# Joins kept clear of GpSimd, two norms in column halves, an earlier copy and count, a store in three parts

## The reference

```python
# layer 0
h = deltanet_mixer(x, ...)   # x @ w_in, conv of 4 taps, silu, a and b gates, chunked gated delta rule
x = layer_norm(ALPHA * x + h, g, b)                  # norm 0
h = (silu(x @ w_gate) * (x @ w_up)) @ w_down         # dense mixer, width 2816
x = layer_norm(ALPHA * x + h, g, b)                  # norm 1
# layer 1
k, v = x @ w_kv;  h = sliding_window_attention(x @ w_q, k, v) @ w_o
x = layer_norm(ALPHA * x + h, g, b)                  # norm 2
h = sum over the top 2 of 8 experts: gate * (silu(x @ w_g[e]) * (x @ w_u[e])) @ w_d[e]
x = layer_norm(ALPHA * x + h, g, b)                  # norm 3, the output

# in the delta rule: (I + L)^-1 for every head and chunk, L strictly lower triangular
def layer_norm(x, g, b):
    mu = mean(x); xc = x - mu
    return xc * rsqrt(mean(xc * xc) + 1e-5) * g + b
```

## Time and profile before

| | us |
|---|---|
| three runs of the kernel before | 1278.57, 1278.9, 1277.63 |
| median | 1278.57 |
| the profiled execution | 1280.17 |
| span of its trace | 1278.3 |
| PE busy | 1253.4 (98%) |
| DVE busy | 1006.0 (79%) |
| ACT busy | 834.4 (65%) |
| GpSimd busy | 97.9 (8%) |
| mean HBM traffic | 293 GB/s |

### The profile page before, as it was taken

How to read it: one execution, slowest core, us unless ns; L and a number is a source line. 1 busy time by engine, 2 the same in 40 slices (tenths; PEclk the granted TensorE clock), 3 DMA queues, 4 the chain that set the end, 5 groups by cost and what they waited for, 6 DMA issues and landing times.

```text
span 1278.3 us, 16890 instructions
## 1 busy us (share of the span) xinstructions
PE 1253.4 (98%) x6773; PEld 1071.1 (84%) x6773; DVE 1006.0 (79%) x855; ACT 834.4 (65%) x842; POOL 97.9 (8%) x116
## 2 busy tenths in 40 slices
PE   8999999999999999999999999999999999999996
PEld 8998998888888987888888888888888888888885
DVE  6877846656645676888888898888898888988897
ACT  5785344454534464677777777777777777777773
POOL 4044201100001100300000000000000000000200
PEclk9999999999999999999999999999999999999998
DMA  9744012997554513899999999999999999999991
GB/s 315 254 147 148 1 34 91 400 367 246 182 197 154 184 59 132 299 386 401 389 389 395 389 385 378 382 386 371 391 386 371 389 387 369 386 394 359 391 397 75
DMA packets 188852, 375.76 MB, mean 294 GB/s; under 512 B 12240, under 2 KB 69696, under 8 KB 188768
## 3 DMA queue, kind: packets, MB, share of 16 engines
q1 hardware_dynamic: 179744, 345.02, 74.5%
q0 software_dynamic: 6864, 25.81, 5.3%
q10 hardware_dynamic: 2160, 3.79, 0.8%
HBM read 354.12 MB, written 20.45 MB: 293 GB/s over the span
## 4 chain that ended last, share of the span: by engine, by line
PE 92%; DVE 3%; DMA 2%; ACT 1%; issue 1%; SPq 1%; POOL 0%; DVEq 0%; ACTq 0%
PE ps L1456 88%; PE ps L1934 1%; DMA raw<-in_moe_w_gu 1%; DVE lo L928 1%; DMA raw<-in_dn_w_in 1%; SPq L301 1%; PE ps L1927 0%; PE ps L1790 0%; ACT hi L555 0%; PE ps L1565 0%; DVE Tm L1113 0%; DVE x L1429 0%; DVE x L964 0%; DVE ps L958 0%; ACT ps L570 0%
## 5 line engine op out<-in xcount | busy, mean ns | idle before, releaser
L928 DVE TENSOR_TENSOR lo<-raw,hi 128x2048 fp32r<-128x2048 f32 x326 | 744.9, 2297 | 181.1 <-ACT hi L555 180.1
L555 ACT ACTIVATE hi<-raw 128x2048 fp32r<-128x2048 f32 x326 | 625.5, 1919 | 290.2 <-PE ps L1456 255.3
L1456 PE MATMUL ps<-hi,xg_hi 128*128 128x512 f32 x704 | 277.6, 394 | 1.3 <-DVE lo L928 1.2
L1456 PE MATMUL ps<-hi,xg_lo 128*128 128x512 f32 x704 | 274.6, 390 | 0.0
L1456 PE MATMUL ps<-lo,xg_hi 128*128 128x512 f32 x704 | 274.1, 389 | 0.0
L1456 PE MATMUL ps<-xT_both,hi 128*128 128x256 f32 (+1 forms) x896 | 224.0, 330 | 2.7 <-DVE xT_both L936 2.1
L1456 PE MATMUL ps<-xT_both,lo 128*128 128x256 f32 x624 | 175.8, 282 | 0.0
L1456 PEld LDWEIGHTS ps<-xT_both,hi 128*128 128x128 f32 x896 | 150.9, 190 | 20.1 <-issue 3.2
L1456 PEld LDWEIGHTS ps<-hi,xg_hi 128*128 128x128 f32 x704 | 132.2, 188 | 29.3 <-DVE lo L928 1.6
L1456 PEld LDWEIGHTS ps<-hi,xg_lo 128*128 128x128 f32 x704 | 132.1, 188 | 28.0
L1456 PEld LDWEIGHTS ps<-lo,xg_hi 128*128 128x128 f32 x704 | 132.3, 188 | 26.5
(11 more groups left out here) (298 smaller groups left out, 1264.4 us busy)
## 6 DMA issues: line engine op xcount, KB each, us to landing
raw<-in_moe_w_gu SPq DMA_DIRECT2D x352, 512.0 KB, 7.4
raw<-in_moe_w_down SPq DMA_DIRECT2D x176, 512.0 KB, 6.6
raw<-in_ffn_w_gu SPq DMA_DIRECT2D x44, 512.0 KB, 8.2
raw<-in_dn_w_in SPq DMA_DIRECT2D x32, 512.0 KB, 8.8
raw<-in_ffn_w_down SPq DMA_DIRECT2D x22, 512.0 KB, 4.0
xe<-xTf POOLq DMA_DIRECT2D x1, 8192.0 KB, 29.0
raw<-in_dn_w_out SPq DMA_DIRECT2D x8, 512.0 KB, 3.8
ys<-xTf POOLq DMA_DIRECT2D x1, 4096.0 KB, 40.1
```

The source lines that it names most:

```text
L555: act.activation(slot(hi, j), slot(raw, j), ACT.Copy).then_inc(hi_ready, 1)
L928: dve.tensor_tensor(slot(lo, j), slot(raw, j), slot(hi, j).bitcast(F32), ALU.subtract).then_inc(lo_ready, 1)
L1456: return pe.matmul(dst, lhsT, rhs, start=start, stop=stop)
```

## The change

- GpSimd waits for `inv_rc` 4, the end of the four joins of level 0, ahead of its product of `conv` and `eG`; the products of `zn` stand behind it in the queue.
- DVE copies a and b out of bank 7 ahead of `project(0)`.
- In the product before norms 0, 1 and 2, PE does block 1 one column half after the other (`last_block`), and counts `block1_half` after the first. `unit_used` of the last unit but one now comes after 18 of the block's 24 products, not after 12.
- `mean(1)` adds the halves one by one, with a sum each, and the small operations take both sums.
- `finish(1)` writes the halves one by one, in norms 0 and 1 (`half_normed`) and in norm 3 (`out_half`). `turn_x` runs 14 unread products and waits for the first half, then for the second.
- DVE reads the count in the last expert (b 1, l 2), no longer at the end. PE runs one unread product there, no longer nine.
- SP stores block 0, then the halves of block 1.

```diff
+            pool.wait_ge(inv_rc, 4)
             pool.wait_ge(g_act, 7)
             pool.wait_ge(kk_mm, 4)
             pool.tensor_tensor(conv[:, 0:H, P:T], conv[:, 0:H, P:T], eG[:, :, :], ALU.mult).then_inc(qg_here, 1)
...
-                            used(last)
+                            for h in range(2):
+                                if h == 0:
+                                    dve.wait_ge(block1_half, i + 1)
+                                else:
+                                    used(last)
+                                link(dve.scalar_tensor_tensor(out=x[:, b, columns_of[h]], in0=x[:, b, columns_of[h]], scalar=ALPHA,
+                                                              in1=ps[:, bank + 2 * b + h, :], op0=ALU.mult, op1=ALU.add,
+                                                              accum_out=lnhalf[:, b, h:h + 1]))
+                            settle()
+                            dve.tensor_scalar(lnmu32[:, b:b + 1], lnhalf[:, b, 0:1], lnhalf[:, b, 1:2], -1.0 / (32 * D),
+                                              ALU.add, ALU.mult).then_inc(ln_mean, 1)
...
+                    if i < 2 and b == 1:
+                        for h in range(2):
+                            dve.scalar_tensor_tensor(out=x[:, b, columns_of[h]], in0=ps[:, bank + 2 * b + h, :], scalar=lnrs[:, b:b + 1],
+                                                     in1=lnb[:, columns_of[h]], op0=ALU.mult, op1=ALU.add
+                                                     ).then_inc(ln_done[b] if h else half_normed, 1)
+                        return
...
-            project(0)
             dve.wait_ge(ab_mm, 1)
             dve.tensor_copy(abT[:, :], ps[0:2 * H, 7, 0:T]).then_inc(ab_here, 1)
+            project(0)
             project(1)
...
+                            if p == 0 and last and b == 1 and l == 2:
+                                dve.wait_ge(route_here, 1)
+                                full = dve.value_load(cint[0:1, 0:1], min_val=0, max_val=T)
...
-            experts(0)
-            full = dve.value_load(cint[0:1, 0:1], min_val=0, max_val=T)
+            full = experts(0)
...
                     if s == 2:
-                        busy(18, 0)
-                    if s % 2 == 0:
+                        busy(14, 0)
+                    if s == 2:
+                        pe.wait_ge(half_normed, norms)
+                    elif s == 0 or s == 3:
                         pe.wait_ge(ln_done[s // 2], norms)
...
+                def last_block(b):
+                    t = slice(b * P, b * P + P)
+                    for i, dst in enumerate(dsts[b]):
+                        for n_, j in enumerate(units):
...
+                                for a, w, p in ((a_hi, w_hi, 0), (a_hi, w_lo, 1), (a_lo, w_hi, 2)):
+                                    last = mm(dst, a[:, k, t], w[:, kk, i * width:(i + 1) * width], False,
+                                              j == units[-1] and kk == nk - 1 and p == 2)
+                            if i == len(dsts[b]) - 1:
+                                last.then_inc(unit_used, 1)
+                        if i == 0:
+                            last.then_inc(block1_half, 1)
...
-            busy(9, 7)
+            busy(1, 7)
...
+                sp_.wait_ge(ln_done[0], i + 1)
+                sp_.dma_start(rows[0], fin[:, 0, :]).then_inc(out_done, 16)
+                sp_.wait_ge(out_half, i - 2)
+                sp_.dma_start(rows[1][:, 0:512], fin[:, 1, 0:512]).then_inc(out_done, 16)
+                sp_.wait_ge(ln_done[1], i + 1)
+                sp_.dma_start(rows[1][:, 512:D], fin[:, 1, 512:D]).then_inc(out_done, 16)
```

More of the change, by code:

```diff
@@ L348, in store @@
             def store(i):
-                for b in range(NB):
-                    sp_.wait_ge(ln_done[b], i + 1)
-                    sp_.dma_start(out[0].rearrange("(b p) d -> b p d", p=P)[b], fin[:, b, :]).then_inc(out_done, 16)
+                rows = out[0].rearrange("(b p) d -> b p d", p=P)
+                sp_.wait_ge(ln_done[0], i + 1)
[4 more added lines that the diff above has]
+                sp_.dma_start(rows[1][:, 512:D], fin[:, 1, 512:D]).then_inc(out_done, 16)
             store(3)
@@ L355, in _ @@
             with sp_.If(full > P):
-                sp_.wait_ge(out_done, 16 * NB)
+                sp_.wait_ge(out_done, 48)
                 experts(1)
                 store(4)
-                sp_.wait_ge(out_done, 32 * NB)
-            sp_.wait_ge(out_done, 16 * NB)
+                sp_.wait_ge(out_done, 96)
+            sp_.wait_ge(out_done, 48)
         @block.gpsimd
@@ L947, in mean @@
                             dve.wait_ge(block0_done, i + 1)
-                        else:
-                            used(last)
-                        step(dve.scalar_tensor_tensor(out=x[:, b, :], in0=x[:, b, :], scalar=ALPHA, in1=pair(bank, b),
-                                                      op0=ALU.mult, op1=ALU.add, accum_out=lnsum[:, b:b + 1]))
+                            step(dve.scalar_tensor_tensor(out=x[:, b, :], in0=x[:, b, :], scalar=ALPHA, in1=pair(bank, b),
+                                                          op0=ALU.mult, op1=ALU.add, accum_out=lnsum[:, b:b + 1]))
+                        else:
+                            for h in range(2):
[9 more added lines that the diff above has]
+                                              ALU.add, ALU.mult).then_inc(ln_mean, 1)
+                            step(dve.tensor_scalar(lnmu[:, b:b + 1], lnhalf[:, b, 0:1], lnhalf[:, b, 1:2], 1.0 / D, ALU.add, ALU.mult))
+                            return
                     dve.tensor_scalar(lnmu32[:, b:b + 1], lnsum[:, b:b + 1], -1.0 / (32 * D), None, ALU.mult).then_inc(ln_mean, 1)
@@ L963, in finish @@
                     dve.wait_ge(ln_rstd, 2 * i + b + 1)
+                    if i < 2 and b == 1:
[3 more added lines that the diff above has]
+                                                     ).then_inc(ln_done[b] if h else half_normed, 1)
+                        return
+                    if b == 1 and i >= 3:
+                        for h in range(2):
+                            dve.scalar_tensor_tensor(out=fin[:, b, columns_of[h]], in0=ps[:, 2 * b + h, :], scalar=lnrs[:, b:b + 1],
+                                                     in1=lnb[:, columns_of[h]], op0=ALU.mult, op1=ALU.add
+                                                     ).then_inc(ln_done[b] if h else out_half, 1)
+                        return
                     dve.scalar_tensor_tensor(out=x[:, b, :] if i < 3 else fin[:, b, :], in0=pair(bank or 0, b), scalar=lnrs[:, b:b + 1], in1=lnb[:, :],
@@ L1396, in turn_of @@
                                     rest_xg(s + 1)
+                    return full if p == 0 and last else None
                 if p:
@@ L1512, in to_tokens @@
                 width = dsts[0][0].shape[1]
+                def last_block(b):
+                    t = slice(b * P, b * P + P)
+                    for i, dst in enumerate(dsts[b]):
+                        for n_, j in enumerate(units):
+                            w_hi = slot(hi, j).rearrange("p (k n) -> p k n", k=nk)
+                            w_lo = slot(lo, j).rearrange("p (k n) -> p k n", k=nk)
+                            for kk in range(nk):
+                                k = k0 + n_ * nk + kk
+                                for a, w, p in ((a_hi, w_hi, 0), (a_hi, w_lo, 1), (a_lo, w_hi, 2)):
[5 more added lines that the diff above has]
+                            last.then_inc(block1_half, 1)
                 for b in range(NB):
+                    if norm_follows and b == NB - 1:
+                        last_block(b)
+                        break
                     t = slice(b * P, b * P + P)
```

8 lines of the change are left out of this document (5 added, 3 removed).

## The result

The changed kernel takes 1271.59 us (median of 9 runs, 1269.59 to 1277.45) beside 1278.57 us for the kernel before (9 runs taken beside them, 1277.63 to 1282.93). The ratio is 0.9946, with a 95% interval from 0.9934 to 0.9958: 6.9 us less, between 5.4 and 8.4. Its profiled execution took 1274.18 us with a span of 1272.4, which is 5.9 us less than the span of the profile before.

A forecast was written before the change was run, and what follows sets the result against it. PE was taken as the bound, carrying 92% of the chain of waits. Terms 1.7 + 3.3 + 0.3 + 0.4 - 0.05 + 1.1 - 0.2 + 0 = 6.55, say 6.5 us, off the 1278.57 median gave 1272.1 us, range 1270.4 to 1274.9.

The forecast's parts named there:

- the likeliest case: Whole kernel: the forecast with its small bounds holds, 1271.0 to 1273.3 us; chance 0.66.
- a and b copied first: Kernel start: PE's 1.69 us wait for the copy of a and b goes; value 1.7 us, bounds 1.0 and 1.7.
- Joins: Inverse: masked copies kept clear of GpSimd's conv product, second(6) starts earlier; gain 3.3 us, bounds 1.6 and 3.4.
- the share that was laid to the low clock: Inverse: beyond 1.9 us for the join, the rest of 3.3 us was the second slow join and PE's low clock.
- the first rival: PE's clock falls anyway, one 3.4 us stretch costing 1.7: 1273.8 us, two 1275.5; chance once or twice 0.12.
- Norms 0 and 1: Block 1, mean and finish in halves: 0.4 us each, bounds 0 and 0.6; 0.3 and 0.4 after the late load.
- Norm 2: Norm before routing: first half worth nothing, a later cut_hi may delay copies of x; -0.05 us, bounds -0.3 and 0.1.
- the clock falls all the same: Rival: PE drops to 1.2 GHz at the inverse or behind norms 0 and 1; 1273.8 or 1275.5 us, chance 0.12.
- The end: After the experts: without the load and with one unread product, sums start 1.1 us sooner; either edit alone gains nothing.
- The register load in the last expert: Reading the count there costs DVE up to 1.3 us amid its cuts; value -0.2 us, bounds -1.3 and 0.
- The rival that was slower than before: Register load in the last expert takes very long, stopping DVE's cuts; at 20 us load 1283.8 us, chance 0.03.
- The store: Final output: three stores carry the same 1 MB as two, the last half as long; value 0, bounds -0.3 and 0.3.

## Why the prediction came true, point by point

The forecast was 1272.1 us, the measured medians are 1271.59 and, later, 1272.77; both lie in the range and in the likeliest case's own range. The ratios give a gain of 5.4 to 8.4 us and, the second time, of 6.4 to 9.9. The parts that repeat from profile to profile sum to 1.7 + 3.25 + 0.6 + 0.6 + 1.0 - 0.5 = 6.7 us, against 6.5 forecast. That the sums lie so near is in part luck: the norms gave 0.5 more than forecast and the load of the count 0.2 more, the store took 0.5 that was not forecast and the end gave 0.1 less.

*a and b copied first*: right in the profile (1.74 for 1.7), no new wait. What the prediction did not know is that the wait is not always there. T stood at 27.29, 27.11, 26.80 and 26.84 in the four profiles with the copy at its old place and the usual start, and PE waited 1.69, 1.49, 1.31 and 1.25 us for the copy, so the gain is 1.3 to 1.7 us, and none after a late start.

*Joins*: right, 3.3 us for 3.3. The step that failed is inside it: the share that was laid to the low clock. The low clock cost nothing there, so that its going could give nothing back. The gain is DVE's, 1.94 + 1.35 us of two shortened copies (2.67 and 2.04 to 0.73 and 0.69), in a stretch in which DVE set the pace. They sum to 3.3 and need no clock. The lower bound of 1.6, and the first rival's price at this place, ask something else, what a fall would cost with the copies short; none came in eight profiles, so no run shows it. Nor does the gap of 1.41 us bring the fall by itself: five other profiles have the gap and no fall behind it. The sentence on the Trainium skill ("SBUF — State Buffer", Who interferes with whom) stands: of the two kinds of copy only the one with two SBUF inputs was slowed (2.68 us against 0.70 in the kernel with the wait moved), as that page has it.

*Norms 0 and 1*: the mechanism was right, the size too small: 0.61 and 0.59 us for 0.3 and 0.4. The term for the halved mean measured 0.53 for 0.3 in the trace of the changed kernel: the first half started 0.1 us earlier than worked out, the second 0.60 behind it instead of 0.67, and the small value 0.73 behind the second instead of 0.8. Of the 0.53, 0.46 reached the next stage. The halved finish gave 0.15 for 0.1. The 0.1 us that the late load behind norm 0 was to take back did not show.

*Norm 2*: the -0.05 for the order of work is too small to be told. With the same low clock, 3.4 us, the stage took 17.27 to 17.29 us with the halves and 17.27 and 17.41 in the old order. What came was the rival "the clock falls all the same", at a place where the prediction had not put it: it looked at the inverse and at norms 0 and 1. The profile before had shown such a stretch in norm 2, and it lay outside the windows that I listed: I had read the windows from 600 us on and the one at 130. It costs 1.0 to 1.7 us each time, in the kernel before as well as after, so it moves single profiles (+1.54 here) more than the comparison of medians.

*The end*: 1.00 for 1.1, and both edits were needed, as said, up to 0.28 us that the fewer unread products bring alone: PE needs only the first low part to begin, and the sentence "the other would have kept it" left that out.

*The register load in the last expert*: -0.2 was too pessimistic and the gap of 1.3 us did not show. The prediction took the 1.3 us idle at the end for a length that the load has wherever it stands. The load takes 0.54 + 0.21 us and runs on DVE's queue beside a cut of 2.29 us that has begun, so neither DVE's 12% to spare nor its idle time was needed. The rival that was slower than before rested on there being no row of the load; the view of the source line shows one, 0.54 us, so a load of 12 us or more had no ground.

*The store*: the term put at 0 measured -0.45, beyond its bound of -0.3. 0.12 us are the finish in two operations, which the prediction named (0.1) but did not carry into the sum, and 0.36 are the longer way from the last issue to the end of the span. The prediction reckoned with a last store that is half as long, 0.7 us less. It landed 3.1 us behind its issue for 3.3 with two stores and 3.2 before, so most of the 0.7 is not there, and what it gained was lost between the landing and SyncE's next step.

The FFN's -0.29 and the experts' -0.41 are not the change's. Over the fourteen profiles the FFN took 183.2 to 184.8 us and the experts 748.1 to 749.7, with kernels of either kind at both ends, and PE's waits for the cuts' low parts there sum to 0.7 us in one and 1.3 in another.

What stays open: why the medians differ by 7.0 and 8.2 us and the repeating parts sum to 6.7. The timed runs leave only a span and a mean clock, so where their low stretches lie can't be told. It is open, too, why PE's clock rises late in some profiles, and what SyncE waits for behind the last landing.

## What to carry to other kernels

Cut two traces at the same events and compare stage by stage: here the inverse, both norms and the attention repeat to 0.1 us from profile to profile, while the total wanders by several, so a change of half a microsecond can be seen in its stage and never in the time. Before a low clock is priced, ask who sets the pace in that stretch: where another engine does it costs nothing, where PE is the one, up to half of its length (in norm 2, 1.0 to 1.7 us for each 3.4). Where the profile puts idle time down to an engine that had long been done, look at the source line of the register load in front of it. Look where a GpSimd operation on SBUF lies beside DVE copies with two SBUF operands, and if its result isn't wanted soon, let it wait until the data comes from PSUM.

## What the runs showed of the hardware

The granted clock's low stretches up to the experts' end are 3.4 or 6.8 us long, one or two to a stage, and how many come in a given stage differs from one execution to the next of the same program (norm 2 of the changed kernel: 6.8 us in one stretch, and 10.2 in two). In norm 2 they came among transposes, the router's small products and unread ones, with PE stopping for no more than 0.33 us; three unread products put in between the router's and three more ahead of them went with 2.4 GHz throughout in both profiles, while three fewer stood behind block 0's. The Trainium skill ("TensorE: Matmul & The Clock Gate", What's actually happening) has the throttled state released by activity; the two kernels with the added products agree.

At the start PE runs its first sixteen transposes in 3.68 us in three profiles and in 1.96 to 2.05 in eleven. The trace's first record of the full clock comes at 10.7 to 11.0 us in the three and at 4.5 to 6.6 in the eleven; a window's 1.00 ahead of the first record says nothing. The longer form costs 1.1 to 1.6 us up to T.

A masked copy of 512 columns with data and mask in SBUF takes 0.73 us alone, 1.42 beside a GpSimd product of 512 columns, and 2.68 beside one of 1024; with its data in PSUM it takes 0.70 to 0.75 beside the same product. The slow copies end 0.6 us behind the GpSimd product that was under way when they began (130.63 behind 130.04 in the kernel before, 128.78 behind 128.19 with the wait moved, 122.86 behind 122.25 in the changed kernel), so their length follows from where the product ends. Where the copy was under way first (124.17 to 124.90 in the changed kernel), it kept its 0.73 us, and the GpSimd product that started beside it at 124.55 took 1.44 us where its like took 1.28. GpSimd pays too: its two products of `zn` took 5.58 us beside the slow copies and 4.69 us clear of them.

A register load from SBUF takes 0.54 us on DVE, and 0.21 for the operation behind it. Behind an instruction that has ended it left DVE idle for 1.31 us; behind a cut of 2.29 us that was running it cost nothing.
